# The sample's channels of two input projections, made by steps and turned by transposes

## The reference, cut to what matters

```python
# layer 0 (even): h is (steps, 1024), w_in is (1024, 3240)
qkv, b_logit, a_logit, z_a, cq, ckv_kr, z_b = split_last(h @ w_in, (1536, 4, 4, 512, 384, 288, 512))
qkv_c, conv_new = causal_dwconv(qkv, conv_buf, conv_w)      # 4 taps along time, one filter per channel
qa, ka, va = split_last(silu(qkv_c), (512, 512, 512))
...
# layer 1 (odd): w_in is (1024, 4096)
q, f, i, z = split_last(h @ w_in, (1024, 1024, 1024, 1024))
fg = lb + (1.0 - lb) * sigmoid(f)
qh, kh, lh = silu(q), 1.0 - fg, log(fg)                     # lh is summed along time within chunks of 64
```

## Time and profile before

| | us |
|---|---|
| median of 3 runs | 3975.02 (3974.63 to 3975.99) |
| the profiled execution | 3975.13 |
| its span, first to last instruction | 3973.4 |
| PE busy | 3766.1 (95%) |
| DVE busy | 1751.5 (44%) |
| ACT busy | 1327.0 (33%) |
| granted clock of PE, mean over the span | 0.978 |

### The profile page before, as it was taken

How to read it: one execution, slowest core, us unless ns; L and a number is a source line. 1 busy time by engine, 2 the same in 40 slices (tenths; PEclk the granted TensorE clock), 3 DMA queues, 4 the chain that set the end, 5 groups by cost and what they waited for, 6 DMA issues and landing times. The chain is left out here.

```text
span 3973.4 us, 58814 instructions
## 1 busy us (share of the span) xinstructions
PE 3766.1 (95%) x22764; PEld 2725.2 (69%) x22764; DVE 1751.5 (44%) x4467; ACT 1327.0 (33%) x3423; POOL 165.4 (4%) x191
## 2 busy tenths in 40 slices
PE   5999999969999888999999998999999999899998
PEld 3777777759999654666666443776777677577775
DVE  2433344445555324655555223112211221399996
ACT  1111111135555223665555101212221222255554
POOL 0000000010100100000000000000000000000000
PEclk8999999989999999999999999999999999899999
DMA  7111111232110110100000555211111111433433
GB/s 284 53 53 50 45 45 53 36 108 81 65 54 20 37 32 30 36 24 16 15 13 6 210 202 188 81 69 69 63 58 69 69 64 59 170 132 127 169 127 114
DMA packets 114800, 317.24 MB, mean 80 GB/s; under 512 B 30040, under 2 KB 48392, under 8 KB 109384
## 3 DMA queue, kind: packets, MB, share of 16 engines
q1 hardware_dynamic: 111864, 288.48, 20.1%
q0 software_dynamic: 2768, 26.47, 2.3%
HBM read 205.16 MB, written 109.74 MB: 79 GB/s over the span
## 5 line engine op out<-in xcount | busy, mean ns | idle before, releaser
L2342 PE MATMUL e_p<-e_hT,w_ahead 128*128 128x128 f32 x3264 | 411.0, 276 | 3.5 <-DMA shared<-w_in_o 3.5
L2342 PEld LDWEIGHTS e_p<-e_hT,w_ahead 128*128 128x128 f32 x3264 | 389.5, 193 | 11.5 <-issue 11.5
L535 PEld LDWEIGHTS a_p<-a_hT,w_even 128*128 128x128 f32 x3264 | 369.3, 193 | 9.4 <-issue 7.6
L535 PE MATMUL a_p<-a_hT,w_even 128*128 128x128 f32 x3264 | 369.5, 276 | 1.3 <-DVE a_hT L318 1.3
L550 PE MATMUL a_p<-w_even,a_hT 128*128 128x512 f32 (+2 forms) x1024 | 370.2, 523 | 0.0
L550 PEld LDWEIGHTS a_p<-w_even,a_hT 128*128 128x128 f32 x1024 | 194.3, 191 | 164.4 <-issue 115.5
L1665 DVE TENSOR_REDUCE q_mx<-q_sps 128x1 f32<-128x512 f32 (+4 forms) x320 | 181.4, 583 | 215.2 <-PE q_sps L1506 214.3
L2734 PE MATMUL h_b<-h_w,h_oT 128*128 128x512 f32 x512 | 236.7, 596 | 0.0
L2189 PE MATMUL c_b<-shared,c_oc 128*128 128x512 f32 x512 | 224.8, 599 | 10.1 <-DMA c_oc<-scr_ob 10.1
L2293 ACT ACTIVATE e_r<-e_p 128x512 f32<-128x512 f32 x66 | 39.4, 597 | 518.3 <-PE e_p L2348 298.8
L1594 ACT ACTIVATE q_P<-q_sps,q_mx 128x512 f32<-128x512 f32 (+4 forms) x320 | 190.7, 603 | 19.6 <-DVE q_mx L1670 14.8
(11 more groups left out here) (457 smaller groups left out, 6252.2 us busy)
## 6 DMA issues: line engine op xcount, KB each, us to landing
scr_qkg<-e_r SPq DMA_DIRECT2D x68, 512.0 KB, 2.6
h_rq<-scr_qkg SPq DMA_DIRECT2D x17, 2048.0 KB, 10.5
scr_iz<-e_r SPq DMA_DIRECT2D x34, 512.0 KB, 2.6
scr_qkv<-a_cv SPq DMA_DIRECT2D x17, 768.0 KB, 3.2
d_sc<-scr_qkv SPq DMA_DIRECT2D x17, 768.0 KB, 4.3
wa<-w_ada SPq DMA_DIRECT2D x8, 1536.0 KB, 16.1
w_ahead<-w_ada POOLq DMA_DIRECT2D x8, 1536.0 KB, 7.6
w_ahead<-w_in_o POOLq DMA_DIRECT2D x6, 2048.0 KB, 9.5
```

Of the source, the lines that this page charges most:

```text
L535: mm = pe.matmul(bank[g][:, (c % 4) * P:(c % 4 + 1) * P], w[:, k, c * P:(c + 1) * P], hT[:, p, k, :], start=k == 0, stop=k == KD - 1)
L2342: mm = pe.matmul(bank[n % 4][:, c * P:(c + 1) * P], w[k][:, a:a + P], hT[:, p, k, :], start=k == 0, stop=k == KD - 1)
```

## The change

For the sample tile alone, the channel blocks are no longer made with 128 weight columns stationary. They are made as the other columns are, with 64 steps stationary and the weight columns moving, two halves of the columns side by side; the result (steps on partitions) is copied from PSUM to `xn`, the left half by ScalarE and the right half by VectorE, so that a 128x128 block of `xn` holds channel block c in its upper 64 rows and another block in its lower 64; a transpose by TensorE turns each into channels by steps, and ScalarE copies or activates the two halves of each to where they stood before. In `in_even` the columns are cut 512+512 and 256+256, with six transposes; the pair of 256 writes both halves of one bank, `xps[1]`. In `in_odd` they are 512+512 twice, `f` first and then `q`, with eight transposes. Only the 64 real steps are written; in `in_odd` the rest of `sg` is set to 0.5 by VectorE.

What moves in `in_odd`: TensorE now waits for all of tile 15's drains before the first pair (before, the first two banks waited for less); `f` is drained before `q`; the Silu of `q` goes behind the two logarithms; so SyncE's store of `q` waits for that, ahead of the other stores in its queue. TensorE no longer waits for ScalarE's drains before the pairs of `i` and of `z`. Seven semaphores are new. The loops over the prompt's tiles stay as they are.

```diff
@@ in_even, ScalarE, the last tile @@
+                if last(t):
+                    act.wait_ge(tok_p, 1)
+                    act.copy(xn[0:DEC, 0:512], bank[0][0:DEC, :]).then_inc(tok_a, 1)
+                    act.wait_ge(tok_p, 2)
+                    act.copy(xn[0:DEC, 512:768], xps[1][0:DEC, 0:256]).then_inc(tok_a, 1)
+                    for first, n, src, need in ((0, 4, xps[0], 2), (8, 2, bank[0], 3)):
+                        act.wait_ge(proj, t * 7 + need)
+                        halves = src[:, 0:n * P].rearrange("p (c e t) -> p e c t", e=2, t=DEC)
+                        for e in range(2):
+                            a = act.copy(xp[:, first + n * e:first + n * e + n, 3:3 + DEC], halves[:, e])
...
@@ in_even, TensorE @@
+            def sample_channels(t, p):
...
+                side_by_side(pe, of(0, 512, bank[0][0:DEC]), of(512, 1024, bank[1][DEC:P]))[1].then_inc(tok_p, 1)
+                side_by_side(pe, of(1024, 1280, xps[1][0:DEC]), of(1280, 1536, xps[1][DEC:P]))[1].then_inc(tok_p, 1)
+                for n, (dst, blocks) in enumerate(((xps[0], 4), (bank[0], 2))):
+                    pe.wait_ge(tok_a, n + 1)
+                    pe.wait_ge(tok_v, n + 1)
+                    for c in range(blocks):
+                        mm = pe.transpose(dst[:, c * P:(c + 1) * P], xn[:, n * 512 + c * P:n * 512 + (c + 1) * P], keep["ident"][:, :])
...
@@ in_even, VectorE, the last tile @@
+                    for n, (src, at, wide) in enumerate(((bank[1], 0, 512), (xps[1], 512, 256))):
+                        dve.wait_ge(tok_p, n + 1)
+                        dve.tensor_copy(xn[DEC:P, at:at + wide], src[DEC:P, 0:wide]).then_inc(tok_v, 1)
                 dve.wait_ge(act_out, t * OUTS + 3)
@@ in_odd, SyncE @@
-                sp.wait_ge(a_out, t * 6 + 2)
+                sp.wait_ge(a_out, t * 6 + (4 if last(t) else 2))
                 sp.dma_start(scr["qkg"][t, :, 0:D], r[:, 0, :]).then_inc(st[0], 16)
@@ in_odd, ScalarE, the last tile @@
+                if last(t):
+                    sample_copies()
+                    act.wait_ge(Gk_r, t)
+                    sample_turned(t, 2, xps[1], sg, ACT.Sigmoid)
...
                 act.activation(flat(sg[:, :, :]), r[:, 1, :], ACT.Ln, bias=tiny[:, 0:1]).then_inc(lk_r, 1)
+                if last(t):
+                    act.wait_ge(st[0], t * 16)
+                    sample_turned(t, 4, xps[0], r[:, 0, :].rearrange("p (h t) -> p h t", t=P), ACT.Silu)
@@ in_odd, TensorE, the last tile @@
+                pe.wait_ge(a_out, t * 6)
+                side_by_side(pe, (bank[2][0:DEC, :], steps, cols(D)), (bank[3][DEC:P, :], steps, cols(D + 512)))[1].then_inc(tok_p, 1)
+                pe.wait_ge(v_out, t * 2)
+                side_by_side(pe, (bank[0][0:DEC, :], steps, cols(0)), (bank[1][DEC:P, :], steps, cols(512)))[1].then_inc(tok_p, 1)
+                turned(0, xps[1])
+                turned(1, xps[0])
+                pe.wait_ge(hTr_r, t + 1)
...
@@ in_odd, VectorE, the last tile @@
-                dve.wait_ge(a_out, t * 6 + 4)
+                if last(t):
+                    for n, b in enumerate((3, 1)):
+                        dve.wait_ge(tok_p, n + 1)
+                        dve.tensor_copy(xn[DEC:P, n * 512:(n + 1) * 512], bank[b][DEC:P, :]).then_inc(tok_v, 1)
+                    dve.wait_ge(Gk_r, t)
+                    dve.memset(sg[:, :, DEC:P], 0.5).then_inc(half, 1)
+                    dve.wait_ge(half, 1)
+                dve.wait_ge(a_out, t * 6 + (2 if last(t) else 4))
```

More of the change, by code:

```diff
@@ L371, in in_even @@
         grow = sb("a_grow", [2 * KD, P])
+        tok_p, tok_a, tok_v = sem("a_tok_p"), sem("a_tok_a"), sem("a_tok_v")
         gate_t, gate_out, gate_st = sem("a_gate_t"), sem("a_gate_out"), sem("a_gate_st")
@@ L479, in step @@
                     act.wait_ge(hist_out, 3 * 16)
-                for g in range(3):
+                if last(t):
[8 more added lines that the diff above has]
+                            a = act.copy(xp[:, first + n * e:first + n * e + n, 3:3 + DEC], halves[:, e])
+                            if e or not first:
+                                a.then_inc(act_out, 1)
+                for g in range(0 if last(t) else 3):
                     act.wait_ge(proj, t * 7 + g + 1)
@@ L511, in _, with of @@
         def _(pe):
+            def sample_channels(t, p):
+                def of(a, b, dst):
+                    return dst[:, 0:b - a], lambda k: hT[:, p, k, 0:DEC], lambda k: w[:, k, a:b]
+                side_by_side(pe, of(0, 512, bank[0][0:DEC]), of(512, 1024, bank[1][DEC:P]))[1].then_inc(tok_p, 1)
[5 more added lines that the diff above has]
+                        mm = pe.transpose(dst[:, c * P:(c + 1) * P], xn[:, n * 512 + c * P:n * 512 + (c + 1) * P], keep["ident"][:, :])
+                        if c >= blocks - 2 + n:
+                            mm.then_inc(proj, 1)
             def sample_groups(t, p):
@@ L528, in step @@
                 pe.wait_ge(S["hT_v"], t + 1)
+                if last(t):
+                    sample_channels(t, p)
+                    sample_groups(t, p)
+                    return
                 for g in range(3):
@@ L537, in step @@
                     mm.then_inc(proj, 1)
-                if last(t):
-                    sample_groups(t, p)
-                    return
                 pe_tr(pe, t + 1)
@@ L2242, in in_odd @@
             sem("e_" + n) for n in ("proj", "a_out", "v_out", "fg", "k", "lf", "G", "lk", "Gk", "hTr", "init"))
+        tok_p, tok_a, tok_v, half = sem("e_tok_p"), sem("e_tok_a"), sem("e_tok_v"), sem("e_half")
         st = [sem(f"e_st{j}") for j in range(6)]
@@ L2297, in drain_sample, with sample_copies, sample_turned @@
                 act.activation(dst[0:DEC], bank[n % 4][(n - 6) * DEC:(n - 5) * DEC, :], ACT.Silu).then_inc(a_out, 1)
-            def step(t, p, i):
[L2300 to L2306, removed]
+            def sample_copies():
+                for n, b in enumerate((2, 0)):
+                    act.wait_ge(tok_p, n + 1)
+                    act.copy(xn[0:DEC, n * 512:(n + 1) * 512], bank[b][0:DEC, :]).then_inc(tok_a, 1)
+            def sample_turned(t, need, src, dst, func):
+                act.wait_ge(proj, t * 8 + need)
+                both = src[:, :].rearrange("p (c e t) -> p e c t", e=2, t=DEC)
+                for e in range(2):
+                    act.activation(dst[:, 4 * e:4 * e + 4, 0:DEC], both[:, e], func).then_inc(a_out, 1)
+            def step(t, p, i):
+                if last(t):
+                    sample_copies()
+                    act.wait_ge(Gk_r, t)
+                    sample_turned(t, 2, xps[1], sg, ACT.Sigmoid)
+                else:
+                    act.wait_ge(st[0], t * 16)
+                    drain(t, 0, part(0, 0), ACT.Silu)
+                    drain(t, 1, part(0, 1), ACT.Silu)
+                    act.wait_ge(Gk_r, t)
+                    drain(t, 2, flat(sg[:, 0:4, :]), ACT.Sigmoid)
+                    drain(t, 3, flat(sg[:, 4:8, :]), ACT.Sigmoid)
                     act_hT(act, t + 1, 1 - p)
@@ L2323, in _, with sample, turned @@
         def _(pe):
+            def sample(t, p):
+                steps = lambda k: hT[:, p, k, 0:DEC]
+                cols = lambda a: lambda k: w[k][:, a:a + 512]
+                own = lambda e: lambda k: w[k][:, 2 * D:3 * D].rearrange("p (j e v) -> p e j v", e=2, v=P)[:, e]
+                by_head = lambda ap: ap.rearrange("p (j v) -> p j v", v=P)
+                def turned(n, dst):
+                    pe.wait_ge(tok_a, n + 1)
+                    pe.wait_ge(tok_v, n + 1)
+                    for c in range(4):
+                        mm = pe.transpose(dst[:, c * P:(c + 1) * P], xn[:, n * 512 + c * P:n * 512 + (c + 1) * P], keep["ident"][:, :])
+                        if c >= 2:
+                            mm.then_inc(proj, 1)
+                pe.wait_ge(a_out, t * 6)
[5 more added lines that the diff above has]
+                pe.wait_ge(hTr_r, t + 1)
+                for mm in side_by_side(pe, (by_head(bank[0][0:DEC, :]), steps, own(0)), (by_head(bank[1][DEC:P, :]), lambda k: hTr[:, k, P - DEC:P], own(1))):
+                    mm.then_inc(proj, 1)
+                for mm in side_by_side(pe, (bank[2][0:DEC, :], steps, cols(3 * D)), (bank[3][DEC:P, :], steps, cols(3 * D + 512))):
+                    mm.then_inc(proj, 1)
             def step(t, p, i):
@@ L2326, in step @@
                 pe.wait_ge(S["hT_v"], t + 1)
-                for n in range(4 if last(t) else 8):
+                if last(t):
+                    sample(t, p)
+                    return
+                for n in range(8):
                     if n % 2 == 0:
@@ L2349, in step @@
                     mm.then_inc(proj, 1)
-                    if n == 3 and not last(t):
+                    if n == 3:
                         pe_tr(pe, t + 1)
[L2352 to L2363, removed]
             pe_tr(pe, 0)
```

## The result

| us | before | after |
|---|---|---|
| median | 3974.82 (3974.10 to 3975.99, 4 runs) | 3951.15 (3948.98 to 3953.68, 4 runs) |
| ratio | 1 | 0.994, 95% interval 0.9923 to 0.9958 |
| the profiled execution | 3975.13 | 3948.98 |
| its span | 3973.4 | 3947.2 |
| PE busy | 3766.1 (95%) | 3743.5 (95%) |

3952.0 was forecast; the kernel is faster by 23.7 us, 0.6%. Measured twice more, with five runs each, it gave 3951.59 (ratio 0.9944, 0.9930 to 0.9958) and 3951.57 (0.9937, 0.9924 to 0.9951); the kernel before, beside them, had medians of 3973.69 and 3973.95, so 22.1 and 22.4 us.

What follows compares the result with a forecast made beforehand. TensorE, busy 95%, was taken to bound `in_odd` to its last product, then ScalarE; two chains within about 1 us end `in_even`. Sum: 3975.13 - 9.4 (`in_even`) - 13.7 (`in_odd`) = 3952.0 us, range 3947.5 to 3959.

Steps and rivals of the forecast that it cites:

- TensorE in `in_even`: End of `in_even`: 21.60 us of channel products replaced by sets of 7.09 and 3.7 us, second pair done at 801.8.
- The copies in `in_even`: After the 256-wide set: PSUM copies, two transposes and ScalarE's copies into `xp` end at 803.6 to 803.8, 9.5 us earlier.
- The wait that then decides: `in_even`: convolution waits for `state_conv` landing at 804.9, about 1.1 us after the copies; Silu at 817.3, 9.4 us gained.
- a convolution released by the load: Sign of being right in `in_even`: convolution starts near 805, released by the `state_conv` load and not by ScalarE.
- `in_odd`: End of `in_odd`: turned channels and a table load of 1.28 us saved; `z` ends at 3427.7 instead of 3441.45, 13.7 us gained.
- The mode of the array: Both stages: a switch there and back fits in 0.2 us; six new switches at that price would lose about 1 us.
- One bank: Rival, `in_even`: halves of the 256 pair don't overlap, set takes 7.1 us, gain 6.1, total 3955.3; chance 0.08.
- Late loads: Rival, `in_even`: `state_conv` lands after 804.9, each us later costs 1 us, up to 3960.3; chance 0.06.
- Pairs that don't overlap: Rival, both stages: channels cost 21.3 and 28.3 us, as much as before; total within 2 us of 3975; chance 0.03.
- The clock falling: Rival, both stages: long half-array work at 1.2 GHz instead of 2.4 takes 51 us more; total 4003; chance 0.02.
- The next stages giving part back: Rival, starts of the next stages: clock rising later costs 2 to 4 us, total about 3955; chance 0.05.
- shifted by a constant: Sign of being right: after `hgrn` starts 23.1 us earlier, the rest of the timeline is shifted by a constant.

Runs made afterwards that it cites:

- odd_only: Kernel before with only `in_odd` changed, `in_even` as before: median 3962.8 us, ratio to before 0.9971.
- conv_twice: Changed kernel with the three `state_conv` loads issued twice, first into a tile nothing reads: 3952.8 us, one run.
- two_banks: Changed kernel with the right half of the 256-wide pair in another bank than the left: 3955.3 us, one run.
- halves_apart: Changed kernel with all eight channel products of the left half ahead of the right half's eight: 3964.53 us, ratio to before 0.9974.
- whole_third: The changed kernel as it is, measured again: median 3951.6 us.

## Why the prediction was right, step by step

**TensorE in `in_even`**: held, a little quicker. The 256-wide set took 3.62 us for the 3.7 read off a straight line; the second pair was done 10.5 us after the first product instead of 10.8.

**The copies in `in_even`**: a little too dear. From the first product to the convolution's release 12.19 us, forecast 12.8 for the copies (803.8 - 791.0). The two copies of 256 took 0.65 us merged instead of 0.74, the two of 128 took 0.46, and those of 256 ran while TensorE still made the last two transposes.

**The wait that then decides**: wrong in kind, though it moved the sum little. I read the landing of `state_conv` off one execution (20.9 us after the last start, 804.9) and let it bind; the sign that I gave for being right, a convolution released by the load, did not come. In every other trace that shows the landing of these loads at that place the slowest took 17.0 to 18.4 us. All nine have `in_even` changed, so they alone don't tell whether the change or the execution made the difference. The stores beside the loads speak for the execution: `scr_z` landed after 12.1 us in the trace of before, after 9.7 in `odd_only`, which has the same `in_even`, and after 9.4 in that of after. So the loads were in time by about 1.5 us in the trace of after.

By the prediction's own terms the wait was worth 0.1 us: without it ScalarE's drains free the Silu at 803.8 + 12.72 + 0.66 = 817.18 (it says 817.1, and 9.6 gained where 9.5 follows), against 817.3 with it. What made 9.97 of 9.4 is the rest of the chain, 0.6 us quicker up to the copies. That each us later than 804.9 would cost one was not run: `conv_twice` made the loads 0.42 us later than the copies, with 0.7 us still to spare, which puts the limit near 1.1 us behind the copies, about where the prediction had it.

**`in_odd`**: held, 13.63 against 13.7. The wait for tile 15's drain cost TensorE 0.78 us (0.8 forecast), the first product to the first of `i` 15.39 (15.35), the transposes hid under the copies as said, the table load fell away, and the six stores of SyncE's queue cost nothing (from the store of `z` to `hgrn` 4.56 us, before 4.57).

**The mode of the array**: the transposes stand between sets of pairs without a gap of their own. From the end of the second set's copies at 3399.75 to the first pair of `i` at 3400.46 there are 0.7 us, which four transposes and their waits fill. A cost shows in one place, at the change from full-array to half-array work at the start of the sample tile in `in_even`: TensorE begins 0.09 us nearer to tile 15's last Silu (above), in every trace with this stage changed. That the change of the array's mode is the cause is argued, not shown.

**The rivals.** *One bank*: refuted by `two_banks`; the rule for row tiles, carried over from the Trainium skill (TensorEngine Tiling (Array Packing), Gotcha 1: PSUM Pressure), does not hold for two column tiles of one bank, 3.62 us either way. *Late loads*: they did not come, in any trace; made late by 0.42 us past the copies, they cost nothing, and later ones were not run. *Pairs that don't overlap*: refuted by the rows of after. *The clock falling*: refuted; the windows with nothing but the new pairs on TensorE (column after POOL is the granted clock), which answer:

```profile
791.00:795.00 4.00, 4.00 (x19) 1.21 (x19) 0.00 (x0) 0.60 (x1) 0.00 (x0) 1.00 0.80 42
...
3391.00:3399.00 8.00, 8.00 (x39) 2.97 (x35) 0.69 (x1) 0.58 (x1) 0.00 (x0) 1.00 0.00 0
```

*The next stages giving part back*: not by the change (`hgrn` and `delta` take no longer behind it, above), but its price was argued badly. I took three runs within 1.4 us as a sign that the stages between are steady. Beside the experiments the kernel before ran from 3969.5 to 3978.7, and the changed one from 3945.75 to 3954.77. The range of 3947.5 to 3959 held the three medians, but not each single run. So the rest of the timeline was not "shifted by a constant": `hgrn` started 25.7 us earlier, not 23.1, with 2.5 us of that from the wander. The two stretches came out by their mechanism, to 0.6 and 0.1 us; that the median lies within 0.9 us of the forecast is partly luck.

## What to carry to other kernels

Where a tile fills only half of the stationary side, turning the product round so that two halves share the array is worth its copies and transposes, if TensorE bounds the stage to its end and most of the copies lie under the next set (in `in_even` those of the last set did not, and 1.7 us stood bare). Measure such a change by the length of the stretch it touches, from one named instruction to another: that repeats to 0.02 us where the total wanders by several. The landing of a DMA is a figure of one execution; an edit that makes it the last to arrive needs it from several.

## What the runs showed of the hardware that was not expected

Products of different column tiles (the left and the right 64 columns of the array) run beside each other even when they stand apart in the program: four records ahead at the border of two halves (3398.42 and 3398.43, rows of `halves_apart`). The Trainium skill (TensorE: Matmul & The Clock Gate, Part 3: Packing small matmuls — row/col tiling) says that matmuls are monotone in program order in start and end; by their recorded starts these are not: the right half's first record starts at 3398.43, and the left half's record of 3398.85, which is ahead of it in the program, after it.

The stages between the two stretches took from 2557.8 to 2568.5 us with the same instructions. In the windows of `delta` up to the next stage, a longer execution goes with a lower granted clock (kernel before, then `whole_third`):

```profile
835.45:1355.90 520.45, 475.40 (x3887) 447.35 (x3887) 268.07 (x800) 278.89 (x927) 50.04 (x41) 0.97 0.19 61
```

```profile
825.13:1349.00 523.87, 478.11 (x3892) 449.22 (x3893) 267.96 (x800) 278.66 (x927) 51.04 (x43) 0.96 0.18 60
```

3.4 us more, of which TensorE's busy time has 2.7, at a mean of 0.96 instead of 0.97 of the full clock. The difference arises early in `delta`. In the 20 us from 15 to 35 us after its first load the granted clock was 0.67 to 0.68 in six of the twelve traces and 0.50 to 0.57 in the other six, so near or at the lower level, 1.2 GHz. The first six need 513.2 to 514.9 us from that load to the start of `delta`'s last VectorE instruction, the others 515.4 to 517.5. The kernel before is among the first, `odd_only`, with the same `in_even`, among the others, and the changed kernel is in both, so it is not the change that decides. Why one execution is granted less than another stays open; no kernel here was made for it.
